# The first block's attention scores from rounded operands, split into leads and rests

## Time and profile before

| | |
|---|---|
| median of 3 runs | 2925.62 us (2921.84 to 2929.99) |
| the profiled execution | 2937.56 us, of which the span is 2935.7 us |
| PE busy | 2773.1 us, 94% |
| PEld / DVE / ACT / POOL busy | 2400.3 / 1339.5 / 953.1 / 916.0 us |
| score products (L659), 128 records | 39.0 to 280.1 us from the span's start |

### The profile page before, as it was taken

How to read it: one execution, slowest core, us unless ns; L and a number is a source line. 1 busy time by engine, 2 the same in 40 slices (tenths; PEclk the granted TensorE clock), 3 DMA queues, 4 the chain that set the end, 5 groups by cost and what they waited for, 6 DMA issues and landing times.

```text
span 2935.7 us, 43494 instructions
## 1 busy us (share of the span) xinstructions
PE 2773.1 (94%) x16616; PEld 2400.3 (82%) x16616; DVE 1339.5 (46%) x2027; ACT 953.1 (32%) x1514; POOL 916.0 (31%) x396
## 2 busy tenths in 40 slices
PE   7999889999869999999999999989998999999999
PEld 5666668888659999888999999989997777888887
DVE  4443352223357786434352322469675434533222
ACT  3333432223332332434232322332323433333222
POOL 2110234444214322111344433434221113444444
PEclk9998879999879999988999999999999989999999
DMA  4211122222212211101222222222111101222223
GB/s 143 61 54 42 50 76 94 93 93 94 71 42 94 80 51 44 52 31 37 68 91 87 94 87 81 93 78 94 51 51 47 42 29 58 94 94 93 94 97 110
DMA packets 61809, 215.35 MB, mean 73 GB/s; under 512 B 8144, under 2 KB 8144, under 8 KB 61648
## 3 DMA queue, kind: packets, MB, share of 16 engines
q1 hardware_dynamic: 56192, 198.80, 20.7%
q10 hardware_dynamic: 5024, 12.82, 1.4%
q0 software_dynamic: 432, 1.43, 0.2%
HBM read 210.85 MB, written 2.16 MB: 73 GB/s over the span
## 4 chain that ended last, share of the span: by engine, by line
PE 55%; issue 24%; POOLq 12%; DVE 5%; ACT 2%; DVEq 2%; ACTq 0%; DMA 0%; SPq 0%; POOL 0%
PE ps L569 15%; PE ps L570 15%; PE ps L571 15%; POOLq L511 11%; PE ps L659 2%; PE ps L672 2%; PE ps L641 1%; PE ps L935 1%; ACT wh L1073 1%; PE ps L552 1%; PE ps L910 1%; DVE arena L1886 1%; PE ps L780 1%; DVE H L1582 1%; DVE arena L1579 1%
## 5 line engine op out<-in xcount | busy, mean ns | idle before, releaser
L510 POOL TENSOR_TENSOR wl<-stage,wh 128x1024 fp32r<-128x1024 f32 x374 | 907.1, 2425 | 1950.2 <-ACT wh L1073 1949.7
L569 PE MATMUL ps<-Uh,wh 128*128 128x264 f32 (+1 forms) x2768 | 945.8, 342 | 32.1 <-DVE Ul L1585 15.8
L570 PE MATMUL ps<-Ul,wh 128*128 128x264 f32 (+1 forms) x2768 | 909.8, 329 | 0.0
L571 PE MATMUL ps<-Uh,wl 128*128 128x264 f32 (+1 forms) x2768 | 907.7, 328 | 2.2 <-issue 2.2
L1073 ACT ACTIVATE wh<-stage 128x1024 fp32r<-128x1024 f32 x374 | 396.8, 1061 | 1489.7 <-PE ps L571 1487.2
L569 PEld LDWEIGHTS ps<-Uh,wh 128*128 128x128 f32 x2768 | 534.7, 193 | 122.3 <-issue 54.6
L571 PEld LDWEIGHTS ps<-Uh,wl 128*128 128x128 f32 x2768 | 533.4, 193 | 43.3
L570 PEld LDWEIGHTS ps<-Ul,wh 128*128 128x128 f32 x2768 | 535.7, 194 | 39.0 <-issue 1.9
L570 PE MATMUL ps<-HIDl,wh 128*128 128x512 f32 (+1 forms) x1024 | 347.5, 339 | 0.0
L571 PE MATMUL ps<-HIDh,wl 128*128 128x512 f32 (+1 forms) x1024 | 346.3, 338 | 0.0
L569 PE MATMUL ps<-HIDh,wh 128*128 128x512 f32 (+1 forms) x1024 | 346.2, 338 | 0.0
(11 more groups left out here) (292 smaller groups left out, 3323.3 us busy)
## 6 DMA issues: line engine op xcount, KB each, us to landing
stage<-w SPq DMA_DIRECT2D x374, 512.0 KB, 3.3
arena<-bias_rows ACTq DMA_DIRECT2D x16, 448.0 KB, 5.0
arena<-w_mla ACTq DMA_DIRECT2D x8, 384.0 KB, 3.1
H<-xT SPq DMA_DIRECT2D x8, 256.0 KB, 6.6
out<-H ACTq DMA_DIRECT2D x8, 256.0 KB, 2.8
arena<-pT SPq DMA_DIRECT2D x1, 512.0 KB, 8.1
arena<-pairs POOLq DMA_DIRECT2D x1, 512.0 KB, 4.1
arena<-causal POOLq DMA_DIRECT2D x1, 320.0 KB, 3.3
```

What stands on the lines that cost most here:

```text
L510: pool.tensor_tensor(wl[:, j, :], stage[:, j, :], wh[:, j, :].bitcast(F32), ALU.subtract).then_inc(w_split, 1)
L569: pe.matmul(dst, w_lead, tok.part(a_lead, h), start=(k == 0), stop=False)
L570: pe.matmul(dst, w_lead, tok.part(a_rest, h), start=False, stop=False)
L571: mm = pe.matmul(dst, w_rest, tok.part(a_lead, h), start=False, stop=(k == len(acts) - 1))
```

## The change

A score becomes two fp32r products that are summed in PSUM. A query tile gets two versions (`qa2`, `qb2`: one for each half). In the version of a half, that half's 64 rows hold the query's lead and the other 64 rows its rest (query less lead). The key tile (`ka2`, `kb2`) holds for each half the key's lead twice, in both groups of 64 rows, and the key's rest stands in tiles of its own (`kal`, `kbl`). The first product of 128 rows gives lead by lead and rest by lead, the second of 64 rows gives lead by key's rest:

```
-                pe.matmul(ps[:, 4 + u, 0:len(keys) * P], q[rows, b * P:(b + 1) * P],
-                          k[rows, keys[0] * P:(keys[-1] + 1) * P], start=True, stop=True).then_inc(s_done[u], 1)
+                pe.matmul(dst, q[:, half, b * P:(b + 1) * P], k[:, half, seen], start=True, stop=False)
+                pe.matmul(dst, q[rows, half, b * P:(b + 1) * P], kl[rows, seen], start=False, stop=True).then_inc(s_done[u], 1)
```

```
+            def query_leads(dst):
+                b = used_up(False)
+                for half in range(2):
+                    rows = slice(64 * half, 64 * half + 64)
+                    act.activation(in_blocks(dst[rows, half, :]), turned(ps[rows, 2 * b, :]), ACT.Copy)
+                act.drain().then_inc(qk_lead, 1)
+                split_weights()
+            def key_leads(dst):
+                b = used_up(False)
+                for half in range(2):
+                    rows = slice(64 * half, 64 * half + 64)
+                    act.activation(dst[rows, half, :], ps[rows, 2 * b, :], ACT.Copy)
+                act.drain().then_inc(qk_lead, 1)
+                for half in range(2):
+                    own, other = slice(64 * half, 64 * half + 64), slice(64 - 64 * half, 128 - 64 * half)
+                    act.activation(dst[other, half, :], dst[own, half, :].bitcast(F32), ACT.Copy)
+                act.drain().then_inc(qk_lead, 1)
+                split_weights()
```

VectorE computes the rests from the same PSUM buffer, waits for the leads first, and it is now VectorE that frees the buffer and raises `qk_split`:

```
+            def query_rests(dst):
+                b, done = take()
+                dve.wait_ge(unit_done[b], done)
+                dve.wait_ge(qk_lead, n.next(qk_lead))
+                for half in range(2):
+                    own, other = slice(64 * half, 64 * half + 64), slice(64 - 64 * half, 128 - 64 * half)
+                    ins = dve.tensor_tensor(dst[other, half, :].rearrange("p (b q) -> p b q", q=P),
+                                            ps[own, 2 * b, :].rearrange("p (b q) -> p b q", q=P)[:, :, ::-1],
+                                            dst[own, half, :].bitcast(F32).rearrange("p (b q) -> p b q", q=P), ALU.subtract)
+                ins.then_inc(unit_free[b], 1)
+                dve.drain().then_inc(qk_split, 1)
```

More of the change, by code:

```diff
@@ L674, in weigh, with phase @@
                 return mm
-            def phase(hd, scored, steps, behind=None):
+            def phase(hd, scored, steps, behind=None, new=0):
                 pe.wait_ge(exp_ready, n.next(exp_ready))
@@ L692, in phase @@
                     if scored is not None:
+                        if b == 0 and new > 0:
+                            pe.wait_ge(qk_split, n.next(qk_split, new))
                         score(scored, b)
@@ L699, in heads @@
                 nothing = iter(())
-                pe.wait_ge(qkv_ready, n.next(qkv_ready, 2))
-                phase(0, 2, unit_of_block())
+                phase(0, 2, unit_of_block(), new=2)
                 phase(1, 3, unit_of_block() if following else nothing, lambda: transpose_values(vbT))
-                if following:
-                    pe.wait_ge(qkv_ready, n.next(qkv_ready))
                 values_copied()
-                phase(2, 0 if following else None, unit_of_block() if following else nothing)
+                phase(2, 0 if following else None, unit_of_block() if following else nothing, new=1 if following else 0)
                 phase(3, 1 if following else None, unit_of_block() if following else nothing)
@@ L718, in _ @@
                     if hd == b == 0:
-                        pe.wait_ge(qkv_ready, n.next(qkv_ready, 2))
+                        pe.wait_ge(qk_split, n.next(qk_split, 2))
                     score(hd, b)
@@ L1212, in nothing @@
                     pass
[L1214 removed]
+                for b in phase(0, lambda: evacuate(vbT, T0, ready=value_ready, split=True)):
                     exp_block(1, b)
@@ L1219, in heads @@
                     exp_block(2, b)
-                for b in phase(2, (lambda: evacuate(qb, T0, flip=True, ready=qkv_ready, split=True)) if following else nothing):
+                for b in phase(2, (lambda: query_leads(qb2)) if following else nothing):
                     exp_block(3, b)
@@ L1223, in heads @@
                         load_biases(1, (2 * t + 10, 2 * t + 11))
-                for b in phase(3, (lambda: evacuate(kb, T0, ready=qkv_ready, split=True)) if following else nothing):
+                for b in phase(3, (lambda: key_leads(kb2)) if following else nothing):
                     if following:
                         exp_block(0, b)
-            evacuate(vaT, T0, ready=qkv_ready, split=True)
+            evacuate(vaT, T0, ready=value_ready, split=True)
             copy_values(va)
@@ L1702, in _, with key_rests @@
             norm(lambda k: col("g_pre_mix", k), T1, HID, Ul2)
-            pass_units(5)
+            def query_rests(dst):
[9 more added lines that the diff above has]
+                dve.drain().then_inc(qk_split, 1)
+            def key_rests(dst, rest):
+                b, done = take()
+                dve.wait_ge(unit_done[b], done)
+                dve.wait_ge(qk_lead, n.next(qk_lead))
+                for half in range(2):
+                    own = slice(64 * half, 64 * half + 64)
+                    dve.tensor_tensor(rest[own, :], ps[own, 2 * b, :], dst[own, half, :].bitcast(F32), ALU.subtract)
+                dve.wait_ge(qk_lead, n.next(qk_lead))
+                dve.sem_inc(passed, 1)
+                dve.drain().then_inc(qk_split, 1)
+                dve.sem_inc(unit_free[b], 1)
             def copy_values(dst):
@@ L1762, in outputs, with phase @@
                                   rinv[:, i, :].unsqueeze(2).to_broadcast([P, QB, DH]), ALU.mult).then_inc(o_free, 1)
-            def phase(hd, t, scored, scored_t, behind=None):
+            def phase(hd, t, scored, scored_t, behind=None, rests=None):
                 copy_exps(hd, 0)
@@ L1772, in phase @@
                     score_block(scored, b)
+                if rests is not None:
+                    rests()
                 outputs(hd, t)
```

62 lines of the change are left out of this document (38 added, 24 removed), and 6 rows, old and new, of the table LOOPS.

## The result

The changed kernel takes 2946.53 us (median of 8 runs, 2942.57 to 2961.00), the kernel before 2928.94 us in as many (2921.84 to 2938.56): a ratio of 1.0068, 95% interval 1.0046 to 1.0089 (it is taken over all executions and isn't quite that of the medians). It is slower by 17.6 us, where +4.9 was forecast. The forecast's range, 2914 to 2943, was built on a median before of 2925.62; on 2928.94 its upper end is 2946.

The account below looks back on a forecast made before the run. TensorE's products were taken to bound the kernel, with ScalarE's chain at phase ends. Rounds +0.5, last round -3.2, start +1.0 and clock +6.6 gave +4.9 us: 2930.5 on the median, range 2914 to 2943.

Parts of the forecast that it names:

- Where the bound lies: Attention phases: TensorE's products bound inside a phase, ScalarE's 2.87 us chain at its end; three of four scores on the path.
- The score's price: A 512-column score with its unit product: 1.20 us (0.43, 0.43, 0.34) instead of 1.39, changes of rows costing time.
- rival 1: Scores: changing rows is nearly free between two products of one kind; 2916 us, faster; chance 0.20.
- Rival 4: Scores: fp32r products take as long as float32, 1.05 us more a score; +58, 2985 us; chance 0.03.
- The chain: ScalarE's copies at phase ends: next transposes 3.3 us behind the unit's end in phases 1 and 2, 4.3 in phase 3.
- The sum by work: Whole kernel without clock effects: rounds +0.5, last round -3.2, start +1.0, together -1.7 us.
- The start: Before the first phase: its value unit waits for a PSUM buffer VectorE frees, 64.65 instead of 62.72; start's sum +1.0 us.
- The clock: Phase boundaries: longer TensorE idle brings six clock dips where there were two, +6.6 us, possible from 0 to +18.
- Rival 2: Phase boundaries: longer idle brings a clock dip at every one; +16, 2942 us, slower; chance 0.25.
- Rivals 3 and 4: Rival 3: VectorE's rests delay `o_free` past the first weighing at nine boundaries, +7, 2937 us, chance 0.07; Rival 4 as above.

Follow-up runs that it names:

- e2: Kernel before, with only the changed kernel's longer ScalarE copy chain added (extra copies into a scratch tile), scores left float32: 2971.6 us.
- e1: Changed kernel, with ScalarE's weight copy and second key copies moved behind the phase's last exponential and VectorE's rests behind outputs: 2929.9 us.
- e3: Changed kernel, with the second score product padded by zeros from 64 to 128 rows: 2904.7 us.
- e10: Changed kernel, with 2, 3, 3, 5 extra products in the boundary idle and the early queries' rests ahead of the last early score: 2912.4 us.
- e8: Kernel before, with 2 extra products into an unused PSUM bank behind the last score of each phase: 2914.5 us.
- e4: Kernel before, with ScalarE's weight copy moved behind the last exponential in every phase that has a unit: 2950.0 us.
- e7: Changed kernel, with 2, 3, 3, 5 extra products into an unused PSUM bank behind the last score of phases 0 to 3: 2919.9 us.
- e9: Kernel before with the changed kernel's long ScalarE chain, plus 2, 3, 3, 5 extra products at the phase boundaries: 2924.5 us.
- e11: The e6 kernel plus 2 extra products behind the last score of each phase: 2875.5 us.
- e5: Changed kernel, with the first dilated queries' rests taken ahead of the second head's last early score: 2941.6 us.
- e6: Changed kernel with the edits of e1, e3 and e5 joined, and the value units' weight copy moved too: 2882.7 us.

## Why the prediction was wrong

- **Where the bound lies** was right: three scores of four on the path, the boundary set by ScalarE's chain. e2 and e1 move the time by the chain and what it does to the clock.
- **The score's price** was right: 1.17 us against 1.20 forecast; rival 1, with changes of rows nearly free, is refuted by 0.41 and 0.42 us a step. The Trainium skill says that a change of the tiling mode drains TensorE (TensorEngine Tiling, Key Properties); the steps here agree, between two products of one type as well. Rival 4 fell with the same steps (its counter-argument named 512-wide products, which the earlier trace rows don't show; e3 has them at 0.23 and 0.24 us).
- **The chain** was right in order and nearly in size: 3.60 and 4.45 us forecast as 3.3 and 4.3; idle 1.45, 2.15, 1.85 and 3.17 us, forecast as 1.4, 1.8, 1.8 and 3.0.
- **The sum by work**, -1.7 us, was right within what can be told: -2.1 between e10 and e8, with -3.6 worked out for e10. A round is 61.3 us to 61.4; +0.2 had been forecast. The trace of e10 gains 2.0 us on that of e8 from the last round on, where 3.2 had been forecast.
- **The start** was right in mechanism and 0.7 us too long, but its clock was left at the price of one dip; in fact 10.2 us at half clock followed (windows 62 to 81.7: 0.74).
- **The clock is the step that failed.** "I expect six dips where there were two: +4 x 1.65 = +6.6." In the profile 9 of the 12 phases from 62 to 264 us are below 1.00, and the stretches behind the start and two key units are two to three times as long as a single dip; in sum some 40 us at half clock against 8. Half clock costs at most half of that, 16 us more than before. The six had no working behind them: the rows showed 2 dips at 13 boundaries with 1.1 us of idle, and nothing for 1.4 to 3.5 us, nor how long a dip lasts behind such a wait. The trace has eight stretches of half clock there, together as long as twelve of the dips before; ten more at the prediction's 1.65 us are 16.5, where it had 6.6. Rival 2, the clock at every boundary, was the case that came true (+16 us given at 0.25; +17.6 measured). That the sizes meet is in part luck: it counted one dip at every boundary, and the trace has fewer but longer ones.
- **Rivals 3 and 4** did not happen: `o_free` made the weighing wait only in the last round, as before.

The bookkeeping, from the medians: filling the boundaries is worth 26.6 us to the changed kernel and 14.4 to the kernel before, so the filling separates them by 12.2; the start's order is worth 7.5 with the rest filled; the work is -2.1. 12.2 + 7.5 - 2.1 = 17.6. This sum had to close, since it goes round through the same five medians; it shares the difference out and doesn't confirm it. Each term carries some 4 us of uncertainty. The traces share out the 14.6 us at the start of the last round in the same way: 12.2 less 3.2 for the filling, 5.9 for the start's order, -0.3 for the work.

**What the profiles and the medians hold beside it.** At the output projection the profile of the kernel after is only 4.0 us behind: its 32 us more of half clock in the rounds stand against 24 less behind them, and this execution of the kernel before lay 8.6 us above its median. And the difference of 18.5 us in span holds two steps of some 9 us in the second block, whose code is the same. The first of them in the timeline of the kernel after:

```profile
1053.70 4.89 DVE L2118 SCALAR_TENSOR_TENSOR arena<-arena,v 128x528 f32<-128x528 f32 x4
...
1055.37 2.66 POOL L522 TENSOR_TENSOR wl<-stage,wh 128x1024 fp32r<-128x1024 f32 x1 [5.29 <-ACT wh L1086]
...
1060.24 1.19 PE L886 MATMUL ps<-arena 128*128 128x128 f32 x4 [6.05 <-DVEq L2126]
```

VectorE's four operations take 4.89 us beside GpSimd's pass, TensorE idles 6.05, and the next products run at half clock. In the kernel before they fell ahead of the pass. Seven other kernels here (e1, e2, e4, e7, e8, e9, e10) show that step too, those with float32 scores among them, and e11 a smaller one; e3, e5 and e6 don't. So it doesn't go with the form of the scores; that it hangs on where the second block falls in time is likely and not shown. From the output projection to the end, where all kernels have the same code, the profiles lose up to 14 us (after) or gain up to 15 (e6) against the kernel before. The medians hold such parts too: e1 is 3.9 us ahead of e7 at the output projection, and its median is 10 us higher. So the place and the mechanism are read from the traces up to the last round, where filling and start order take the changed kernel from 14.6 us behind to 3.5 ahead; the sizes by medians are known only to such a part.

## What to carry to other kernels

Price a longer chain by what the idle does to TensorE's clock, not by its own length: here a chain that costs 10 us with the clock held cost 41 without, and a few products into an unused bank, put in the idle, took the 31 back, of which the traces place some 17 in the rounds. A second product with fewer rows isn't cheaper: padding it with zeros to the rows of its neighbours saved 0.39 us a score. And when work is moved off a chain, look at which engine it starts later, since in e4 GpSimd's pass, fallen on a SBUF-only operation of VectorE, turned an expected gain of some 10 us into a loss of 21.

## What was not expected of the hardware

- The length of idle that the clock bears isn't fixed: in the kernel after it held behind 2.15 us of idle PE at 163.7 us (0.99 in the phase behind it) and fell behind the same 2.15 us at 96.8 and 228.7 (0.89, 0.90); behind 1.1 us it had fallen at 2 of 13 boundaries of the kernel before. Each time TensorE had been busy through the phase before.
- An addition of two 128x4 tiles in SBUF, begun beside GpSimd's pass over 128x1024, ended when the pass did: it took 2.23 us where it came early in the pass (e4), 0.27 to 0.74 where late (the kernel before), and 0.16 beside none. Subtractions that read PSUM took 1.39 us for two both ways.
- A 64-row product between 128-row ones cost 0.39 us more than the same product padded to 128 rows (1.17 us from the lead to the second unit product, against 0.78). How much of it is the weight load that is no longer hidden wasn't separated.
